# Sums of squares of the last attention: one f32 pass, or two float32r passes over a rounded part and its rest

## What is computed

```python
def rms_norm_2(x, gain):
    xf = x.astype(jnp.float32)
    y = xf * lax.rsqrt(jnp.mean(xf * xf, axis=-1, keepdims=True) + RMS_EPS)
    return (y * gain.astype(jnp.float32)).astype(x.dtype)

q_nope = rms_norm_2(q[..., :MLA_QK_NOPE], q_nope_norm)
q_pe = rotary(rms_norm_2(q[..., MLA_QK_NOPE:], q_pe_norm), pos)
k_nope = rms_norm_2(kv[..., :MLA_QK_NOPE], k_nope_norm)
sc = (jnp.einsum('bqhd,bkhd->bhqk', qn, k_nope) + jnp.einsum('bqhr,bkr->bhqk', qp, k_pe)) * scale
a = jax.nn.softmax(jnp.where(causal_mask(i, s), sc, NEG_INF), axis=-1)
out = jnp.einsum('bhqk,bkhv->bqhv', a, v)
```

## Time and profile before

| | |
|---|---|
| median of 3 runs | 3014.52 us (3010.95 to 3014.73) |
| the profiled execution | 3012.53 us |
| its span, first to last instruction | 3010.7 us |
| busy: PE, DVE, ACT, POOL | 96%, 60%, 30%, 10% of the span |
| chain that ended last | PE 88%, DVE 7%, ACT 3%, issue 2% |
| mean granted TensorE clock | 0.989 |

### The profile page before, as it was taken

One profiled execution on the slowest core, in us unless ns is written; L12 is line 12 of the kernel. 1 busy time (PEld: TensorE's weight loads), 2 busy tenths in 40 slices (PEclk: granted clock), 3 DMA queues, 4 the chain that ended last, 5 costly groups with the idle time before them and its releaser, 6 DMA issues.

```text
span 3010.7 us, 36545 instructions
## 1 busy us (share of the span) xinstructions
PE 2897.0 (96%) x12794; PEld 2213.7 (74%) x12802; DVE 1802.4 (60%) x2790; ACT 904.5 (30%) x1606; POOL 294.6 (10%) x213
## 2 busy tenths in 40 slices
PE   8999989998999999998999999999889999999999
PEld 6777857776676888875767688887667768788887
DVE  6775356885445555356466777746755544777646
ACT  2111023343433111033354333202355540333202
POOL 1111003342140111000000011100000000011100
PEclk9999999999999999999999999999999999999999
DMA  4335322121122222322221222332211102222332
GB/s 150 110 110 122 100 80 79 64 71 53 46 83 71 92 96 94 96 81 82 86 78 58 77 98 91 99 96 77 88 42 36 36 28 92 83 91 98 98 95 94
DMA packets 78549, 249.86 MB, mean 83 GB/s; under 512 B 8840, under 2 KB 15368, under 8 KB 78440
## 3 DMA queue, kind: packets, MB, share of 16 engines
q1 hardware_dynamic: 65232, 229.74, 23.3%
q10 hardware_dynamic: 13208, 18.71, 2.4%
HBM read 238.32 MB, written 9.96 MB: 82 GB/s over the span
## 4 chain that ended last, share of the span: by engine, by line
PE 88%; DVE 7%; ACT 3%; issue 2%; DMA 0%; ACTq 0%; POOL 0%; SPq 0%; DVEq 0%; POOLq 0%
PE ps L317 25%; PE ps L318 24%; PE ps L319 24%; PE ps L3387 1%; PE ps L3432 1%; PE ps L3408 1%; PE ps L3409 1%; PE ps L907 1%; PE ps L2904 1%; DVE w_lo L300 1%; PE ps L2180 1%; DVE w_hi L291 1%; PE ps L2889 1%; PE ps L1547 1%; PE ps L2159 1%
## 5 line engine op out<-in xcount | busy, mean ns | idle before, releaser
L317 PE MATMUL ps<-xh,w_hi 128*128 128x512 f32 x2152 | 883.2, 410 | 33.3 <-DVE xl L487 13.5
L318 PE MATMUL ps<-xl,w_hi 128*128 128x512 f32 x2152 | 855.6, 398 | 0.0
L319 PE MATMUL ps<-xh,w_lo 128*128 128x512 f32 x2152 | 854.8, 397 | 0.0
L291 DVE CAST w_hi<-raw 128x1024 fp32r<-128x1024 f32 (+1 forms) x438 | 302.4, 690 | 743.9 <-PE ps L319 706.8
L317 PEld LDWEIGHTS ps<-xh,w_hi 128*128 128x128 f32 x2152 | 406.9, 189 | 172.9 <-issue 56.9
L300 DVE TENSOR_TENSOR w_lo<-raw,w_hi 128x1024 fp32r<-128x1024 f32 (+1 forms) x386 | 502.4, 1302 | 28.5
L318 PEld LDWEIGHTS ps<-xl,w_hi 128*128 128x128 f32 x2152 | 407.5, 189 | 99.8 <-issue 8.9
L319 PEld LDWEIGHTS ps<-xh,w_lo 128*128 128x128 f32 x2152 | 406.7, 189 | 99.5
L317 PE MATMUL ps<-ah,w_hi 128*128 128x512 f32 x704 | 278.3, 395 | 0.0
L319 PE MATMUL ps<-ah,w_lo 128*128 128x512 f32 x704 | 278.3, 395 | 0.0
L318 PE MATMUL ps<-al,w_hi 128*128 128x512 f32 x704 | 278.2, 395 | 0.0
(11 more groups left out here) (429 smaller groups left out, 3707.6 us busy)
## 6 DMA issues: line engine op xcount, KB each, us to landing
raw<-in_ffn_up SPq DMA_DIRECT2D x90, 512.0 KB, 3.3
raw<-in_conv_up SPq DMA_DIRECT2D x88, 512.0 KB, 3.2
raw<-in_ffn_down SPq DMA_DIRECT2D x32, 512.0 KB, 3.5
raw<-in_conv_down SPq DMA_DIRECT2D x32, 512.0 KB, 3.5
raw<-in_merge SPq DMA_DIRECT2D x24, 512.0 KB, 3.2
raw<-in_ple_gate SPq DMA_DIRECT2D x24, 512.0 KB, 3.2
raw<-in_diff SPq DMA_DIRECT2D x24, 512.0 KB, 3.3
raw<-in_mla SPq DMA_DIRECT2D x20, 512.0 KB, 3.2
```

Source lines behind the costliest of these rows:

```text
L291: dve.tensor_copy(self.w_hi[s][:, 0:n], self.raw[r][:, 0:n]).then_inc(self.sem["slot_hi"], 1)
L317: pe.matmul(out, wh, xh, start=start, stop=False)
L318: pe.matmul(out, wh, xl, start=False, stop=False)
L319: return pe.matmul(out, wl, xh, start=False, stop=stop)
```

## The change

Each tile of squares in `tmp` is now split by DVE in a rounded float32r part `sq_hi` and the rest `sq_lo` (`split_square`, two instructions), and PE adds up both with rounded ones (`sums`, made once from the f32 ones) in two float32r matmuls. `sum_squares` waits for the split, ACT's `square` may overwrite `tmp` once the split two before is done, and the new buffers take room that a smaller DMA scratch area gives.

```diff
+        self.sums = [sb(f"sums{r}", [P, P], F32R) for r in range(2)]
+        self.sq_hi = [sb(f"sq_hi{r}", [P, T], F32R) for r in range(2)]
+        self.sq_lo = [sb(f"sq_lo{r}", [P, T], F32R) for r in range(2)]
...
     def sum_squares(self, pe, r, name):
         k, n = self.k, self.normed[(r, name)]
-        pe.wait_ge(*self.on("norm_sq", n))
+        pe.wait_ge(*self.on("sums_lo", n))
...
+        ones = k.sums[name == "PE"][:]
...
-        pe.matmul(k.ps[:, 7, :], k.half_ones if name == "PE" else k.ones, k.tmp[n % 2][:], start=True, stop=True
-                  ).then_inc(k.sem["norm_sum"], 1)
+        pe.matmul(k.ps[:, 7, :], ones, k.sq_hi[n % 2][:], start=True, stop=False)
+        pe.matmul(k.ps[:, 7, :], ones, k.sq_lo[n % 2][:], start=False, stop=True).then_inc(k.sem["norm_sum"], 1)
...
         act.wait_ge(*self.made((r, name)))
         if n >= 2:
-            act.wait_ge(*self.on("norm_sum", n - 2))
+            act.wait_ge(*self.on("sums_lo", n - 2))
...
+    def split_square(self, dve, r, name):
+        k, n = self.k, self.normed[(r, name)]
+        dve.wait_ge(*self.on("norm_sq", n))
+        if n >= 2:
+            dve.wait_ge(*self.on("norm_sum", n - 2))
+        dve.tensor_copy(k.sq_hi[n % 2][:], k.tmp[n % 2][:]).then_inc(k.sem["sums_hi"], 1)
+        dve.wait_ge(*self.on("sums_hi", n))
+        dve.tensor_tensor(k.sq_lo[n % 2][:], k.tmp[n % 2][:], k.sq_hi[n % 2][:].bitcast(F32), ALU.subtract
+                          ).then_inc(k.sem["sums_lo"], 1)
...
     def vector(self, dve):
         k = self.k
+        for sums, ones in zip(k.sums, (k.ones, k.half_ones)):
+            dve.tensor_copy(sums[:], ones).then_inc(k.sem["sums_made"], 1)
         k.round_both(dve, self.w, 0, 2)
+        self.split_square(dve, 0, "K0")
         self.after.rotary_keys(dve)
+        self.split_square(dve, 0, "Q0")
         self.norm_out(dve, 0, "K0")
...
                     if name in ("V3", "PE", "K1"):
                         k.round_both(dve, self.w, 0, at_slot + 2)
                         at_slot += 1
+                    if name[0] != "V":
+                        self.split_square(dve, r, name)
                 if at == self.ROT_UNIT[r % 2 == 0]:
                     self.rope(dve, r)
...
-    nc = bacc.Bacc("TRN2", target_bir_lowering=False, num_devices=1)
+    nc = bacc.Bacc("TRN2", target_bir_lowering=False, num_devices=1, dynamic_dma_scratch_size=4096)
```

More of the change, by code:

```diff
@@ L140 @@
  resid_scaled resid_dve
- conv0 conv1 conv2 silu gate_scaled up_scaled
+ sums_hi sums_lo sums_made conv0 conv1 conv2 silu gate_scaled up_scaled
  norm_sq norm_sum norm_log norm_rstd norm_out
@@ L3279, in plan @@
         u, five = range(self.UNITS), range(len(normed))
-        self.e = k.events(1, product=[key for key in order if key not in self.ends], norm_sq=five, norm_sum=five, norm_log=five, norm_rstd=five,
-                          norm_out=five, v_out=range(len(values)), rope_rot=range(self.PAIRS),
+        self.e = k.events(1, product=[key for key in order if key not in self.ends], norm_sq=five, sums_hi=five, sums_lo=five, norm_sum=five,
+                          norm_log=five, norm_rstd=five, norm_out=five, sums_made=range(2), v_out=range(len(values)), rope_rot=range(self.PAIRS),
                           rope_made=range(3 * self.PAIRS), logits=u, row_min=u, probs_raw=u, row_recip=u, probs=u,
@@ L3593, in vector @@
         k = self.k
+        for sums, ones in zip(k.sums, (k.ones, k.half_ones)):
+            dve.tensor_copy(sums[:], ones).then_inc(k.sem["sums_made"], 1)
         k.round_both(dve, self.w, 0, 2)
+        self.split_square(dve, 0, "K0")
         self.after.rotary_keys(dve)
+        self.split_square(dve, 0, "Q0")
         self.norm_out(dve, 0, "K0")
+        self.split_square(dve, 0, "K1")
         self.norm_out(dve, 0, "Q0")
         k.round_both(dve, self.w, 0, 3)
+        self.split_square(dve, 0, "PE")
         self.norm_out(dve, 0, "K1")
+        self.split_square(dve, 0, "Q1")
         self.norm_out(dve, 0, "PE")
```

## The result

The changed kernel takes 3035.63 us (median of 6 runs, 3033.2 to 3037.11) against 3014.62 us before (6 runs). The ratio is 1.0069, with a 95% interval from 1.0056 to 1.0082: 21 us slower. The forecast was 3032. The profiled execution has a span of 3031.4 us, 20.7 more than before.

What follows compares the result with a forecast made beforehand. The prediction took PE as the bound, busy 228.80 of the unit loop's 230 us. 3012.5 us, +16 (13.1 + 1.7 + 1) for waits less savings, +3.4 for TensorE's clock, gave 3032; forecast 3025 to 3036, 8-in-10 range 3015 to 3041.

Steps and rivals of the forecast that it cites:

- B: K0 of an even round: DVE's gain delays the split; PE waits 1.45 + 0.45 = 1.9 us.
- D: K1 of an even round: rounding, split, then rope hold up the sum by 1.55 us; next logits lose 0.35 more.
- three signs of being wrong: PE's waits for L3583 under 18 us, matmul pair over 0.6 us, or the 230 us unit loop done under 236.
- A: K1 of an odd round: split behind DVE's slot rounding; PE waits 2.5 + 0.45 = 2.9 us, row maximum 1.1 late.
- C: PE's tile of an even round: split behind the rounding; PE waits 0.9 + 0.45 less 0.35, 1.0 us.
- E: Q0 of an odd round: split after the square, ACT later after D; PE waits 0.45 + 0.25, 0.7 us.
- F: PE's tile of an odd round: split behind the rounding; PE waits 0.45 us.
- the start: Start of the last attention: first sum waits for a split, keys' rotary work queues behind; +1 us, bounds -2 to +4.
- The rival of the clock: In the last attention TensorE's clock falls at every A, or also at B and D: 3036 to 3041 us; chance 0.2.
- The cancelling case: In the loop, waits of 6.4 us a pair against 4.5 saved nearly cancel: 3014 to 3020 us; chance 0.15.
- the faster one: In the loop, shorter sums decide and only A is felt: 3006 us, or 2995 with A covered; chance 0.08.
- The no-saving rival: At the sums, two float32r passes cost as much as the f32 one: 3034 us or a little above; chance 0.04.

Runs made afterwards that it cites:

- wait-only kernel: The changed kernel with its old f32 sum over tmp back, still waiting for the split, which nobody reads; 3039.38 us, ratio 1.0086 to the kernel before.
- the one with DVE's work alone: The changed kernel with the old f32 sum waiting for the square alone, while DVE makes its splits for nobody; 3026.45 us, ratio 1.0038.
- saving-only kernel: The changed kernel without DVE's split: ACT writes squares to a float32r tile that PE sums twice, the rest left out; 3006.71 us, ratio 0.9974.

## Why the prediction was right

*The place and the mechanism held.* All of the loss is in this attention, and it is PE waiting for L3583, with the longest steady wait at K1 of odd rounds: 2.65 us against 2.75 to 2.9. B had 1.90 to 1.93 (1.9 forecast), D 1.54 and 0.29 for the logits (1.55 and 0.35). In all PE waited 33.8 us for split and rope, 28.0 without the first sum; 31 were forecast. None of the forecast's three signs of being wrong came. The wait-only kernel, the one with DVE's work alone and the one with the later rounding show that these waits are the cause and that DVE's order makes them. They also show what was added at each wait, forecast as 0.45 us: from the wait-only to the changed kernel A goes from 2.25 to 2.66, B from 1.51 to 1.90, D from 1.15 to 1.54, about 0.4 each.

*Too large were the small ones.* C waited 0.18 (once 0.67) instead of 1.0, E 0.18 to 0.33 instead of 0.7, F 0.21 to 0.23 instead of 0.45. The profile counts a wait from the modelled end of the matmul before, about 0.17 us after PE could have gone on, so part of this is still paid.

*The saving was too large as well.* It was read as 0.92 - 0.47 = 0.45 us a sum, with the two float32r matmuls 0.23 us apart. At A in the changed kernel they start 0.33 apart and the next follows 0.56 behind the first. From the last matmul of the logits to the one behind the sum it was 0.97 us before (to 2235.38) and is 0.57 in the saving-only kernel:

```profile
2234.41 0.22 PE L3410 MATMUL ps<-maskc 128*128 128x128 bf16 x1
...
2234.01 0.22 PE L3416 MATMUL ps<-maskc 128*128 128x128 bf16 x1
...
2234.58 0.27 PE L3424 MATMUL ps<-consts,sq 128*128 128x128 f32 x1
```

So a sum saves 0.40 us, 4.0 a pair and 16 in all. With this the pairs add up. The saving-only kernel waits 2.0 us a pair more than before (2.33 against 0.33) and saves 4.0, and its pair is 2.0 shorter. The changed kernel waits 7.3 more by the profile's count, some 8 with the 0.17 that each wait lacks, and saves 4.0: 4.1 longer.

*The total is in part luck.* The terms of the sum beside what they measured, in the profiled executions. The clock's part in the pairs is their length beyond 75.9; at the start and at the end it is an estimate, half of the time that PE worked at half clock.

| term, us | forecast | measured |
|---|---|---|
| three pairs | 13.1 | 12.2 |
| the last A and the tail | 1.7 | 1.4 |
| the start | 1 | 0.6 |
| TensorE's clock | 3.4 | 8.1 |
| ahead of the attention | 0 | -1.7 |
| together | 19.2 | 20.6 (span: 20.7) |

The last attention begins 1.7 us earlier in the changed kernel, though the work ahead of it is the same in both: the kernel before ran at half clock from 682.9 to 686.3 us, and the changed one did not.

*The clock was the mis-sized term.* Forecast were falls at two of four As, 3.4 us, with 6.8 as the bound. There were five new ones: behind the 2.34 us that PE waits for the first sum of round 1 (1.55 before), behind B twice, behind D once and behind the last A. The other three As held the clock through 2.65 us. The size of one fall was right, 1.6 to 1.7 us; where it stands ahead of another wait, some of it comes back: the first pair is 2.5 us longer for two falls, the third 1.1 for one. At the start PE also works longer at half clock behind the first sum, before and changed (us, PE busy, granted clock, DMA share, GB/s):

```profile
2191.55:2194.96 3.41, 3.41 (x7) 0.50 0.00 0
...
2190.69:2196.65 5.96, 5.92 (x13) 0.50 0.00 0
```

That is another 1.3 us. Without these two the start's 3.6 us are 0.6, near the +1 of the walk.

*One sentence was wrong, though the sum did not show it*: "whatever shortens PE's work counts in full". 228.80 of 230 us busy says that PE had hardly any slack, not that nothing else was as long. The saving-only kernel gave 7.7 us of 16: 2.0 of 4.0 us a pair. The loss of the other half was in the walk without being seen as such: the 0.45 us added at each wait, "since PE arrives earlier by what the sum before saved, while the chain from row maximum to square mostly does not", is that second chain. Hence a right total from waits of 8.85 and a full saving of 4.5; the same total, told properly, is 6.0 of waits and 2.0 of saving.

*The rivals.* The rival of the clock, 3036 to 3041, was right that B and D are long enough for a fall, which no row had shown, and wrong that it would come at every A, where it came once in four. Its clock term, 6.8 or more, was nearer than the forecast's, and the measured 3035.6 lies at its lower edge. The cancelling case and the faster one would have needed waits of 6.4 or less beside a full saving. The rows' own differences were nearly right, 6.0, but the full saving was not to be had. The no-saving rival is off by the saving-only kernel, though its 3034 came nearer to the time than the forecast's 3032.

## What to carry to other kernels

Before giving work from a bound engine's instruction to a half idle one, look at where the new instruction stands in that engine's fixed order and who then waits. Here 45 us of "free" DVE work made the kernel 21 us slower, and moving the rounding of the slot one unit later took 15 of them back. An engine that is 99% busy can have a second chain of equal length beside it; to see it, compute when each operand would be ready if the busy engine came earlier. If a saving comes out half as large as it should, look for a long instruction pair in that chain that could stand one step later: here the same edit was worth 0.7 us a pair before the saving and 2.9 after it.

## What the runs showed of the hardware that was not expected

TensorE's granted clock can fall behind a wait of 1.5 to 2 us, and hold through a longer one. Behind the first B's 1.90 us the matmuls went on at full spacing for 1.5 us and behind the third B's 1.92 for 0.8, and then at 0.43 us a pass, the 1.2 GHz level, for some 3.4 us. Behind D's 1.54 the fall came 1.9 us after the sum, with the 0.29 us for the logits in between. The stretch behind the first B, and the one behind the A with 2.66 us of waiting (us, PE busy, granted clock, DMA share, GB/s):

```profile
2264.70:2268.30 3.60, 3.60 (x10) 0.53 0.01 2
...
2238.70:2242.00 3.30, 3.30 (x16) 1.00 0.39 149
```

The matmuls behind the first B, from the full to the half clock:

```profile
2264.47 0.40 PE L322 MATMUL ps<-cqh,w_lo 128*128 128x512 f32 x1
2264.71 0.44 PE L320 MATMUL ps<-cqh,w_hi 128*128 128x512 f32 x1
...
2265.38 0.63 PE L322 MATMUL ps<-cqh,w_lo 128*128 128x512 f32 x1
...
2265.80 0.63 PE L320 MATMUL ps<-cqh,w_hi 128*128 128x512 f32 x1
```

The kernel's loop is the same in each pair, and yet the clock fell behind B in the first and third pair and not in the second. Whether a given wait costs its length or up to 1.7 us more could not be told from the wait alone. No run here was made to find what decides it, and it stays open.
